# Key pages of the samples issued by SyncE between weights and value pages, in place of GpSimd

## Chip, cores and metric

The kernel runs on one core of a Trainium2 chip. The time is the device time of one execution in microseconds. Engines are called TensorE (PE), VectorE (DVE), ScalarE (ACT), GpSimd (POOL) and SyncE (SP); PEld is TensorE's loading of weights.

## The reference

One step of a decoder with two layers, for a prompt of 512 positions and 8 samples of one position each. Layer 0 mixes by gated linear attention and retention. Layer 1, in which the change lies, mixes by stick-breaking attention (8 heads of 128) and a gating of positions. For the samples the keys and values of the 2048 past positions come from a paged cache, 16 pages of 128 positions a sample:

```python
k_past = cache_k[i][page_table].reshape(dec_b, n_past, HC, DC)
v_past = cache_v[i][page_table].reshape(dec_b, n_past, HC, DC)
...
z = (jnp.einsum('bqhd,bshd->bhqs', q, k) * (q.shape[-1] ** -0.5)
     + offset.astype(jnp.float32)[None, :, None, None])
mask = (k_pos[None, :] < q_pos[:, None])[None, None]
log_beta = jax.nn.log_sigmoid(z)
log_rest = jnp.where(mask, jax.nn.log_sigmoid(-z), 0.0)
between = lax.cumsum(log_rest, axis=3, reverse=True) - log_rest
weight = jnp.where(mask, jnp.exp(log_beta + between), 0.0)
return jnp.einsum('bhqs,bshd->bqhd', weight, v)
```

All of it is in float32. A page of keys or of values, for all 8 heads, is 128 x 1024 numbers, 512 KB; there are 128 pages of each.

## The kernel before

**Projections.** A weight tile of 2048 x 128 is loaded in two halves of 512 KB (a half tile, 8 chunks of 128 rows). ScalarE casts each to `w_hi` (line 986) and VectorE subtracts to get `w_lo` (line 1384); this pair of operations is the split. TensorE multiplies `w_hi` by both parts of the activations and `w_lo` by one, 48 matmuls of 260 columns a half tile (line 558). `w_hi` and `w_lo` have two buffers each, so the split of half tile u waits for TensorE to finish u-2. The raw weights lie in a ring of four slots (`RING`, slots 1 to 4 of `raw`): SyncE loads half tile u+4 when u has been split (lines 375 and 376).

**Stages.** `ada0`, `ra` and `l0` (layer 0), `out0`, then `l1a` (4 passes of 8 half tiles: queries and one gate branch of layer 1), `l1b` (8 passes of 10 half tiles, one head a pass), `out1` (8 passes). The engines run the same order of half tiles, and between them the steps of a generator `mix`, in `l1b` the function `mix1` that each engine has its own version of.

**Samples.** Sample b's keys are multiplied by its queries on VectorE, in `key_page` (line 1773: eight multiply-and-sum instructions a page, one a head). That is done for sample 0 during `l1a`, at the steps of `KEYS0_AT`, and for sample i+1 during pass i of `l1b`, two pages at each step of `KEYS_AT`. The weighted sum of sample i's values runs on TensorE in pass i, two pages at each of the steps 3 to 10 (`value_pages(i, k)`, k from 0 to 7, at the end of the step; sixteen short matmuls of 256 columns). Pages of keys have three slots (`key_slot(p)` is p % 3), pages of values three others.

```python
KEYS0_AT = [23, 24, 24, 25, 25, 28, 28, 29, 30, 30, 31, 33, 33, 34, 34, 35]
KEYS_AT = [1, 3, 4, 5, 7, 8, 9, 10]
```

VectorE's semaphore `k_free` counts finished key pages, TensorE's `v_free` finished value pages. A page p of 3 or more is loaded once page p-3 is finished; the first three pages of a sample wait for the last pages of the sample before.

**Who loads.** SyncE issues the weights and the value pages, in the order of `l1b_pass`: a weight half tile at each `at_` from 0 to 9, value pages 1, 2, 0 at 0, and value pages 2at-3 and 2at-2 from 3 on. GpSimd issues the key pages, in order, and between them the queries of the sample (`queries`), the position weights (`head_weights`) and their bias (`head_bias`) of the head before. Each queue executes in its order: an instruction that waits holds all behind it.

In `walk` VectorE splits, in the turn of half tile u of `l1b`, half tile u+2, and takes the next step of `mix` behind it. ScalarE's `mix1` and TensorE's are interleaved in the same way; TensorE takes step k ahead of half tile k from step 2 on.

Of the kernel before, what the change touches and what calls it, by code (L numbers as in the profile page):

```python
# [24 lines left out]
NPAGE, PAGE, NPOOL = 16, 128, 160  # L25
# [23 lines left out]
L1A_ORDER = [TILE] * 4  # L49
# [18 lines left out]
KEYS0_AT = [23, 24, 24, 25, 25, 28, 28, 29, 30, 30, 31, 33, 33, 34, 34, 35]  # L68
KEYS_AT = [1, 3, 4, 5, 7, 8, 9, 10]
# [54 lines left out]
def build(nc, a, o, cst):  # L124
    ctx = ExitStack()
    with ctx:
        def sb(name, shape, dt=F32):
            return ctx.enter_context(nc.sbuf_tensor(name, shape, dt))
# [3 lines left out]
        def s(name):  # L132
            if name not in sems:
                sems[name] = ctx.enter_context(nc.semaphore(name))
            return sems[name]
# [22 lines left out]
        def region(n):  # L158
            at = used[0]
            used[0] += n  # L160
            assert used[0] <= 16600, used[0]
            return arena[:, at:at + n]
# [53 lines left out]
        qb = region(1024)  # L216
# [16 lines left out]
        ptab = sb("ptab", [1, NB * NPAGE], I32)  # L233
# [76 lines left out]
        def key_slot(p):  # L310

            return p % 3

        def key_buffer(slot):

            return raw[:, 0, :] if slot == 2 else pages[:, slot, :]

        def value_slot(p):

            return 2 + p % 3  # L320
# [38 lines left out]
        def _(sp):  # L359
# [19 lines left out]
            def load_tile(name, i, u, hh, w, col, turns=None):  # L379
                load(name, i, u, w[:, 8 * hh:8 * hh + 8, bass.ds(col, P)], turns)  # L380

            def load_mod(name, i, u, n, w, col, turns=None):
                load(name, i, u, w[:, 2 * n:2 * n + 2, bass.ds(col, 512)], turns)

            def weights(name, i, order, w_tile, tile_cols, mods=(), turns=None):
                seen = {TILE: 0, MOD: 0}
                for u in phases[name][3]:
                    kind = order[u // 2]
                    n = seen[kind]
                    seen[kind] += 1  # L390
                    if kind is TILE:
                        load_tile(name, i, u, n % 2, w_tile, tile_cols[n // 2], turns)
                    else:
                        w_mod, col = mods[n // 8]
                        load_mod(name, i, u, n % 8, w_mod, col, turns)

            v = {k: a[k][0].rearrange("(c p) n -> p c n", p=P)
                 for k in ("e_w_ada", "o_w_ada", "e_w_in", "o_w_in", "e_w_out", "o_w_out")}
# [17 lines left out]
            n = 24  # L416
# [31 lines left out]
            with sp.Fori(1, 8) as j:  # L448
                weights("out0", j, OUT_ORDER, v["e_w_out"], [j * 256, j * 256 + P], turns=(1, 8))

            def l1a_cols(j):
                return [(O_Q if j < 2 else O_VD) + (j % 2) * 512 + P * t for t in range(4)]

            for u in range(8):
                t, hh = OUT_FIRST[u] if u < 4 else (u // 2, u % 2)
                load_tile("l1a", 0, u, hh, v["o_w_in"], l1a_cols(0)[t])
            for j in range(1, 4):
                weights("l1a", j, L1A_ORDER, v["o_w_in"], l1a_cols(j))

            cv = a["cache_v"][0].rearrange("n s h d -> n s (h d)")  # L460

            def l1b_load(i, u):
                col = (O_K, O_V, O_GD, O_U, O_G)[u // 2]
                load_tile("l1b", i, u, u % 2, v["o_w_in"], i * P + col, (1, 8))

            def out1_load(u):
                t, hh = OUT1_FIRST[u]
                load("out1", 0, u, v["o_w_out"][:, 8 * hh:8 * hh + 8, P * t:P * t + P], None)

            def value_page(b, p):  # L470
                first = isinstance(b, int) and b == 0
                if p >= 3:
                    sp.wait_ge(s("v_free"), b * 16 + (p - 2))
                elif not first:
                    sp.wait_ge(s("v_free"), b * 16 - (0, 2, 1)[p])
                page = sp.value_load(ptab[0:1, bass.ds(b * NPAGE + p, 1)], min_val=0, max_val=NPOOL - 1)
                sp.dma_start(pages[:, value_slot(p), :], cv[bass.ds(page, 1)].rearrange("n s d -> (n s) d"))\
                    .then_inc(s(f"page{value_slot(p)}"), 16)

            def l1b_pass(i, last=False):  # L480
                for at_ in range(10):
                    if at_ < 6:
                        l1b_load(i, at_ + 4)
                    elif not last:
                        l1b_load(i + 1, at_ - 6)
                    else:
                        out1_load(at_ - 6)
                    if at_ == 0:
                        for p in (1, 2, 0):
                            value_page(i, p)  # L490
                    if at_ >= 3:
                        for p in (2 * at_ - 3, 2 * at_ - 2):
                            if p < NPAGE:
                                value_page(i, p)

            sp.wait_ge(s("ptab"), 16)
            for u in range(4):
                l1b_load(0, u)
            for i in range(8):
                l1b_pass(i, i == 7)  # L500
            with sp.Fori(1, 8) as j:
# [1508 lines left out]
        def layer1_pages(pool):  # L2010

            pool.wait_ge(s("ptab"), 16)
            pool.wait_ge(s("st_out"), 128)
            pool.wait_ge(s("s_out"), 128)
            ck = a["cache_k"][0].rearrange("n s h d -> n s (h d)")

            def key_page(b, p):
                first = isinstance(b, int) and b == 0
                page = pool.value_load(ptab[0:1, bass.ds(b * NPAGE + p, 1)], min_val=0, max_val=NPOOL - 1)
                if p >= 3:  # L2020
                    pool.wait_ge(s("k_free"), b * 16 + (p - 2))
                    pool.sem_inc(s("pool_waited"), 1)
                elif not first:
                    pool.wait_ge(s("k_free"), b * 16 - (0, 2, 1)[p])
                    pool.sem_inc(s("pool_waited"), 1)
                pool.dma_start(key_buffer(key_slot(p)), ck[bass.ds(page, 1)].rearrange("n s d -> (n s) d"))\  # L2026
                    .then_inc(s(f"key{key_slot(p)}"), 16)

            def queries(b):
                pool.dma_start(qb, q_dram[bass.ds(b, 1), :].rearrange("b n -> (b n)").partition_broadcast(P))\  # L2030
                    .then_inc(s("qb"), 16)

            def head_weights(h):
                if not (isinstance(h, int) and h == 0):
                    pool.wait_ge(s("oc"), h)
                    pool.sem_inc(s("pool_waited"), 1)
                pool.dma_start(ws, a["o_w_s"][0, bass.ds(h, 1)].rearrange("g t s -> t (g s)")).then_inc(s("ws_in"), 16)

            def head_bias(h):
                if not (isinstance(h, int) and h == 0):  # L2040
                    pool.wait_ge(s("gated"), h)
                    pool.sem_inc(s("pool_waited"), 1)
                if not (isinstance(h, int) and h == HC - 1):
                    pool.wait_ge(s("qb"), h * 32 + 32)
                    pool.sem_inc(s("pool_waited"), 1)
                pool.dma_start(brow[:, 0:P], a["o_b_s"][0, bass.ds(h, 1), :].rearrange("b n -> (b n)")
                               .partition_broadcast(P)).then_inc(s("qb"), 16)

            def sample_keys(b):
                for p in range(NPAGE):  # L2050
                    key_page(b, p)
                    if p == 1:
                        if isinstance(b, int) and b == 0:
                            pool.wait_ge(s("q_out"), 16)
                        if not (isinstance(b, int) and b < 2):
                            pool.wait_ge(s("qb"), b * 32 - 16)
                            pool.sem_inc(s("pool_waited"), 1)
                        queries(b)
                        if not (isinstance(b, int) and b == 0):
                            head_weights(b - 1)  # L2060
                    if p == 3 and not (isinstance(b, int) and b == 0):
                        head_bias(b - 1)

            sample_keys(0)
            sample_keys(1)
            with pool.Fori(2, NB) as b:
                sample_keys(b)
            head_weights(HC - 1)
            pool.wait_ge(s("qb"), 32 * HC - 16)
            head_bias(HC - 1)  # L2070
# [143 lines left out]
```

## Time and profile before

| | |
|---|---|
| time, median of 3 runs | 2187.14 us (2185.31 to 2188.33) |
| profiled execution | 2186.84 us, its span 2184.6 us |
| TensorE busy | 2080.9 us, 95% of the span |
| VectorE busy | 1151.6 us, 53% |
| ScalarE busy | 616.9 us, 28% |
| GpSimd busy | 201.7 us, 9% |
| moved by DMA | 445.40 MB, 204 GB/s in the mean |
| key pages | 128 of 512 KB, issued by GpSimd |
| value pages | 128 of 512 KB, issued by SyncE |

The span is the profiled time between the first and the last instruction. Busy time of an engine leaves out register, semaphore and DMA-issuing instructions. Idle time of an engine costs only where the end hangs on it.

### The profile page before, as it was taken

The numbers are of one execution on the slowest core, as the hardware profiler recorded it, in microseconds if no ns is written. First come the engines' busy times: TensorE is split into PE (matmuls) and PEld (weight loads), VectorE is DVE, ScalarE is ACT, GpSimd is POOL, SyncE is SP. The second block draws the span as 40 slices with busy tenths as digits, with TensorE's granted clock in tenths as the row PEclk, the third lists the DMA queues.
The fourth block names the chain that finished last, engine by engine and source line by source line (L and its number), as shares of the span: only waits on it lengthen the run. The fifth ranks groups of instructions, "written<-read, shape, count | busy, mean of one in ns | idle before, by whom it ended". The sixth has DMA issues, their size and how long they took to land.

```text
span 2184.6 us, 44372 instructions
## 1 busy us (share of the span) xinstructions
PE 2080.9 (95%) x16767; PEld 1841.3 (84%) x16767; DVE 1151.6 (53%) x3629; ACT 616.9 (28%) x793; POOL 201.7 (9%) x319
## 2 busy tenths in 40 slices
PE   6889999999999999899969998999999999998998
PEld 2258898988888888799969998888888888888997
DVE  1442544434454454644462277687777677745332
ACT  1422122121221212322233353323323323323221
POOL 0000101101010110100000011111111111000101
PEclk9989999999999999999989999999999999999999
DMA  9977665566675657343333367898898798763442
GB/s 324 305 224 251 194 196 183 186 193 214 192 215 180 209 181 224 103 117 112 113 139 87 108 193 256 288 296 283 285 308 291 257 311 286 229 201 92 131 133 64
DMA packets 401520, 445.40 MB, mean 204 GB/s; under 512 B 17141, under 2 KB 307279, under 8 KB 399808
## 3 DMA queue, kind: packets, MB, share of 16 engines
q1 hardware_dynamic: 359270, 311.99, 46.3%
q0 software_dynamic: 32288, 122.64, 16.1%
q10 hardware_dynamic: 9810, 8.73, 1.2%
q8 instruction: 97, 1.59, 0.3%
q14 instruction: 55, 0.44, 0.1%
HBM read 416.70 MB, written 26.61 MB: 203 GB/s over the span
## 4 chain that ended last, share of the span: by engine, by line
PE 80%; DVE 9%; ACT 4%; DMA 4%; issue 2%; SPq 0%; DVEq 0%; POOLq 0%; ACTq 0%; POOL 0%
PE pt L558 64%; PE m L558 13%; ACT arena L986 2%; DVE arena L1773 2%; DVE w_lo L1384 2%; ACT w_hi L986 2%; PE m L562 2%; DMA raw<-in_e_w_ada 1%; DMA arena<-in_o_k_norm_g 1%; DMA arena<-in_cache_v 1%; PE pt L562 1%; DVE arena L1943 1%; DMA arena<-in_cache_k 0%; DVE arena L1504 0%; DVE act_lo L1466 0%
## 5 line engine op out<-in xcount | busy, mean ns | idle before, releaser
L558 PE MATMUL pt<-act_hi,w_hi 128*128 128x260 f32 x4384 | 905.9, 288 | 29.1 <-DVE act_lo L1471 11.9
L558 PE MATMUL pt<-act_hi,w_lo 128*128 128x260 f32 x4384 | 887.0, 284 | 0.0
L558 PE MATMUL pt<-act_lo,w_hi 128*128 128x260 f32 x4384 | 885.8, 284 | 0.0
L1384 DVE TENSOR_TENSOR w_lo<-raw,w_hi 128x1024 fp32r<-128x1024 f32 x274 | 335.6, 1225 | 819.1 <-ACT w_hi L986 818.0
L558 PEld LDWEIGHTS pt<-act_hi,w_hi 128*128 128x128 f32 x4384 | 678.5, 190 | 90.9 <-issue 69.5
L558 PEld LDWEIGHTS pt<-act_lo,w_hi 128*128 128x128 f32 x4384 | 680.2, 190 | 0.0
L558 PEld LDWEIGHTS pt<-act_hi,w_lo 128*128 128x128 f32 x4384 | 680.1, 190 | 0.0
L986 ACT ACTIVATE w_hi<-raw 128x1024 fp32r<-128x1024 f32 x274 | 289.9, 1058 | 1104.1 <-PE pt L558 1088.2
L986 ACT ACTIVATE arena<-arena 128x1040 f32<-128x1040 f32 (+8 forms) x191 | 158.1, 837 | 164.4 <-DVE arena L1877 57.7
L1773 DVE CUSTOM_DVE_ANT_0 arena<-arena 128x128 f32<-128x128 f32 x704 | 155.1, 288 | 22.9 <-DMA arena<-in_cache_k 16.7
L558 PE MATMUL m<-raw,cond 128*9 128x512 f32 x768 | 131.2, 641 | 16.5 <-DMA raw<-in_e_w_ada 14.2
L558 PE MATMUL m<-arena 128*128 128x256 f32 (+6 forms) x704 | 115.4, 380 | 1.5 <-DVE arena L1617 1.5
L558 PEld LDWEIGHTS m<-arena 128*128 128x128 f32 (+4 forms) x704 | 74.5, 166 | 35.5 <-issue 18.5
L558 PEld LDWEIGHTS m<-raw,cond 128*9 128x9 f32 x768 | 16.6, 90 | 80.2 <-DMA raw<-in_e_w_ada 43.7
L1773 DVE CUSTOM_DVE_ANT_0 raw<-raw,arena 128x128 f32<-128x128 f32 x320 | 71.0, 288 | 13.0 <-DMA raw<-in_cache_k 13.0
L2026 POOL DMA_DIRECT2D arena<-in_cache_k x88 | 46.7, 531 | 334.5 <-DVE arena L1773 153.9
L562 PE MATMUL m<-c_ident,arena 128*128 128x128 f32 (+2 forms) x403 | 57.7, 275 | 19.0 <-DMA c_fold<-const_fold 8.9
L2113 POOL TENSOR_SCALAR arena<-arena 128x256 f32<-128x256 f32 x56 | 51.8, 925 | 226.2 <-DVE arena L1610 192.1
L558 PE MATMUL m<-arena,mod 128*8 128x256 f32 x1024 | 67.8, 380 | 2.5 <-ACT mod L986 1.5
L986 ACT ACTIVATE arena<-m 128x512 f32<-128x512 f32 (+2 forms) x93 | 49.8, 572 | 63.1 <-PE m L558 48.4
L562 PEld LDWEIGHTS m<-c_ident,arena 128*128 128x128 f32 (+2 forms) x403 | 44.7, 142 | 21.6 <-DMA c_fold<-const_fold 8.9
L558 PEld LDWEIGHTS m<-arena,ones 128*128 128x128 f32 x156 | 26.3, 196 | 24.3 <-issue 15.6
(174 smaller groups left out, 1209.7 us busy)
## 6 DMA issues: line engine op xcount, KB each, us to landing
arena<-in_cache_v SPq DMA_DIRECT2D x128, 512.0 KB, 5.2
raw<-in_o_w_in SPq DMA_DIRECT2D x112, 512.0 KB, 5.7
raw<-in_e_w_in SPq DMA_DIRECT2D x98, 512.0 KB, 4.6
raw<-in_e_w_ada SPq DMA_DIRECT2D x96, 512.0 KB, 5.7
raw<-in_o_w_ada SPq DMA_DIRECT2D x96, 512.0 KB, 5.2
arena<-in_cache_k POOLq DMA_DIRECT2D x88, 512.0 KB, 5.6
raw<-in_cache_k POOLq DMA_DIRECT2D x40, 512.0 KB, 5.6
raw<-in_e_w_out SPq DMA_DIRECT2D x32, 512.0 KB, 3.8
```

What stands on the lines that cost most here:

```text
L558: return pe.matmul(out, lhsT, rhs, start=start, stop=stop, skip_group_check=True)
L562: return pe.transpose(out, x, ident[0:k, 0:k])
L986: return act.activation(out, x, fn, **kw)
L1384: tt(w_lo[:, b, :], raw[:, sl, :], w_hi[:, b, :].bitcast(F32), ALU.subtract)\
L1773: last = dve.tensor_tensor_reduce(kpage, kpage, qb[:, P * h:P * h + P], 1.0, 0.0, ALU.mult, ALU.add, to[:, 8 * p + h:8 * p + h + 1])
L1943: tt(z, z, m012[:, 0:SB_ALL], ALU.subtract).then_inc(s("lw"), 1)
L2026: pool.dma_start(key_buffer(key_slot(p)), ck[bass.ds(page, 1)].rearrange("n s d -> (n s) d"))\
L2113: pool.tensor_scalar(carry[:, n, :], S[:, (n - 1) % 2, :], small[:, 6 * (n // 2) + n % 2:6 * (n // 2) + n % 2 + 1], None, ALU.mult).then_i ...
```

## The change

GpSimd's `key_page` goes to SyncE's queue. In `l1b_pass` the key pages of sample i+1 stand behind the weight load and ahead of the value pages of the same `at_` (but behind value pages 1, 2, 0 at 0): pages 0, 1, 2 at 0, and page p at `KEYS_AT[(p - 3) // 2]`, so 3 and 4 at 1, 5 and 6 at 3, 7 and 8 at 4, 9 and 10 at 5, 11 and 12 at 7, 13 and 14 at 8, 15 at 9. The pages of sample 0 stand between the loads of `l1a` and of the first half tiles of `l1b`. GpSimd keeps queries, position weights and bias, and issues those of a sample when all key pages of the sample before are finished. Slots, waits of each page and the work on the engines stay.

```diff
@@ -448,6 +448,32 @@
             with sp.Fori(1, 8) as j:
                 weights("out0", j, OUT_ORDER, v["e_w_out"], [j * 256, j * 256 + P], turns=(1, 8))
 
+            ck = a["cache_k"][0].rearrange("n s h d -> n s (h d)")
+
+            def key_page(b, p):
+                if p >= 3:
+                    sp.wait_ge(s("k_free"), b * 16 + (p - 2))
+                elif b > 0:
+                    sp.wait_ge(s("k_free"), b * 16 - (0, 2, 1)[p])
+                page = sp.value_load(ptab[0:1, b * NPAGE + p:b * NPAGE + p + 1], min_val=0, max_val=NPOOL - 1)
+                sp.dma_start(key_buffer(key_slot(p)), ck[bass.ds(page, 1)].rearrange("n s d -> (n s) d"))\
+                    .then_inc(s(f"key{key_slot(p)}"), 16)
+
+            def keys0(n):
+
+                if n == 16:
+                    sp.wait_ge(s("ptab"), 16)
+                    sp.wait_ge(s("st_out"), 128)
+                    sp.wait_ge(s("s_out"), 128)
+                for p in range(NPAGE):
+                    if n == (16 if p < 3 else KEYS0_AT[p - 3] * 8 // 9 + 6):
+                        key_page(0, p)
+
+            def keys1(b, at_):
+                for p in range(NPAGE):
+                    if at_ == (0 if p < 3 else KEYS_AT[(p - 3) // 2]):
+                        key_page(b, p)
+
             def l1a_cols(j):
                 return [(O_Q if j < 2 else O_VD) + (j % 2) * 512 + P * t for t in range(4)]
 
@@ -455,7 +481,9 @@
                 t, hh = OUT_FIRST[u] if u < 4 else (u // 2, u % 2)
                 load_tile("l1a", 0, u, hh, v["o_w_in"], l1a_cols(0)[t])
             for j in range(1, 4):
-                weights("l1a", j, L1A_ORDER, v["o_w_in"], l1a_cols(j))
+                for u in range(8):
+                    load_tile("l1a", j, u, u % 2, v["o_w_in"], l1a_cols(j)[u // 2])
+                    keys0(8 * j + u)
 
             cv = a["cache_v"][0].rearrange("n s h d -> n s (h d)")
 
@@ -485,17 +513,21 @@
                         l1b_load(i + 1, at_ - 6)
                     else:
                         out1_load(at_ - 6)
+                    if i == 0:
+                        keys0(32 + at_ + 4)
                     if at_ == 0:
                         for p in (1, 2, 0):
                             value_page(i, p)
+                    if not last:
+                        keys1(i + 1, at_)
                     if at_ >= 3:
                         for p in (2 * at_ - 3, 2 * at_ - 2):
                             if p < NPAGE:
                                 value_page(i, p)
 
-            sp.wait_ge(s("ptab"), 16)
             for u in range(4):
                 l1b_load(0, u)
+                keys0(32 + u)
             for i in range(8):
                 l1b_pass(i, i == 7)
             with sp.Fori(1, 8) as j:
@@ -2012,20 +2044,6 @@
             pool.wait_ge(s("ptab"), 16)
             pool.wait_ge(s("st_out"), 128)
             pool.wait_ge(s("s_out"), 128)
-            ck = a["cache_k"][0].rearrange("n s h d -> n s (h d)")
-
-            def key_page(b, p):
-                first = isinstance(b, int) and b == 0
-                page = pool.value_load(ptab[0:1, bass.ds(b * NPAGE + p, 1)], min_val=0, max_val=NPOOL - 1)
-                if p >= 3:
-                    pool.wait_ge(s("k_free"), b * 16 + (p - 2))
-                    pool.sem_inc(s("pool_waited"), 1)
-                elif not first:
-                    pool.wait_ge(s("k_free"), b * 16 - (0, 2, 1)[p])
-                    pool.sem_inc(s("pool_waited"), 1)
-                pool.dma_start(key_buffer(key_slot(p)), ck[bass.ds(page, 1)].rearrange("n s d -> (n s) d"))\
-                    .then_inc(s(f"key{key_slot(p)}"), 16)
-
             def queries(b):
                 pool.dma_start(qb, q_dram[bass.ds(b, 1), :].rearrange("b n -> (b n)").partition_broadcast(P))\
                     .then_inc(s("qb"), 16)
@@ -2046,25 +2064,25 @@
                 pool.dma_start(brow[:, 0:P], a["o_b_s"][0, bass.ds(h, 1), :].rearrange("b n -> (b n)")
                                .partition_broadcast(P)).then_inc(s("qb"), 16)
 
-            def sample_keys(b):
-                for p in range(NPAGE):
-                    key_page(b, p)
-                    if p == 1:
-                        if isinstance(b, int) and b == 0:
-                            pool.wait_ge(s("q_out"), 16)
-                        if not (isinstance(b, int) and b < 2):
-                            pool.wait_ge(s("qb"), b * 32 - 16)
-                            pool.sem_inc(s("pool_waited"), 1)
-                        queries(b)
-                        if not (isinstance(b, int) and b == 0):
-                            head_weights(b - 1)
-                    if p == 3 and not (isinstance(b, int) and b == 0):
-                        head_bias(b - 1)
-
-            sample_keys(0)
-            sample_keys(1)
+            def sample(b):
+                first = isinstance(b, int) and b == 0
+                if first:
+                    pool.wait_ge(s("q_out"), 16)
+                else:
+                    pool.wait_ge(s("k_free"), b * 16)
+                    pool.sem_inc(s("pool_waited"), 1)
+                if not (isinstance(b, int) and b < 2):
+                    pool.wait_ge(s("qb"), b * 32 - 16)
+                    pool.sem_inc(s("pool_waited"), 1)
+                queries(b)
+                if not first:
+                    head_weights(b - 1)
+                    head_bias(b - 1)
+
+            sample(0)
+            sample(1)
             with pool.Fori(2, NB) as b:
-                sample_keys(b)
+                sample(b)
             head_weights(HC - 1)
             pool.wait_ge(s("qb"), 32 * HC - 16)
             head_bias(HC - 1)
```

## Rows read from the trace of the kernel before

**Rows 1.** Busy time of each engine in a regular pass and in the longest.

```profile
core 0: us, PE busy (x) PEld busy (x) DVE busy (x) ACT busy (x) POOL busy (x), PEclk, DMA share, GB/s
...
1420.01:1500.30 80.29, 79.72 (x679) 69.88 (x680) 60.80 (x314) 26.65 (x35) 10.27 (x19) 1.00 0.88 288
...
1741.50:1823.93 82.43, 79.68 (x679) 69.75 (x679) 61.93 (x325) 26.23 (x34) 10.28 (x19) 1.00 0.87 291
```

**Rows 2.** Waits, 1100 to 1990 us: us in total, times, longest.

```profile
DVE arena L1773 <- DMA arena<-in_cache_k: 16.7, 12, 1.9
...
PE m L558 <- DMA arena<-in_cache_v: 1.0, 2, 0.6
```

**Rows 3.** Timeline of SyncE's issues: start us, us, line, transfer, how many.

```profile
1427.20 2.01 SPq L477 DMA_DIRECT2D arena<-in_cache_v  x2
...
1459.98 1.48 SPq L477 DMA_DIRECT2D arena<-in_cache_v  x2
...
1477.32 0.34 SPq L477 DMA_DIRECT2D arena<-in_cache_v  x1
```

**Rows 4.** Timeline of TensorE, passes 0 and 1; in brackets the idle time before.

```profile
1333.50 0.49 PE L558 MATMUL m<-arena,c_from_key 128*128 128x128 f32 x2 [2.91 <-DVE arena L1884]
...
1353.87 1.05 PE L558 MATMUL m<-arena,mod 128*8 128x256 f32 x16
...
1425.81 1.05 PE L558 MATMUL m<-arena,mod 128*8 128x256 f32 x16
...
1433.99 1.05 PE L558 MATMUL m<-arena,mod 128*8 128x256 f32 x16
...
1451.67 1.05 PE L558 MATMUL m<-arena,mod 128*8 128x256 f32 x16
...
1465.51 1.05 PE L558 MATMUL m<-arena,mod 128*8 128x256 f32 x16
...
1482.85 1.05 PE L558 MATMUL m<-arena,mod 128*8 128x256 f32 x16
```

**Rows 5.** Chain that ended last: two half tiles, start us, us.

```profile
1335.21 7.28 PE pt L558 x48
...
1459.64 5.94 PE pt L558 x48
```

**Rows 6.** Timeline of VectorE, and ScalarE's cast at 1425.98.

```profile
1351.55 1.23 DVE L1384 TENSOR_TENSOR w_lo<-raw,w_hi 128x1024 fp32r<-128x1024 f32 x1 [2.85 <-ACT w_hi L986]
...
1425.98 1.06 ACT L986 ACTIVATE w_hi<-raw 128x1024 fp32r<-128x1024 f32 x1 [1.42 <-PE pt L558]
...
1428.62 1.22 DVE L1384 TENSOR_TENSOR w_lo<-raw,w_hi 128x1024 fp32r<-128x1024 f32 x1
...
1430.84 0.28 DVE L1773 CUSTOM_DVE_ANT_0 raw<-raw,arena 128x128 f32<-128x128 f32 x1
...
1434.23 0.08 DVE L1773 DVE_READ_ACCUMULATOR2_ANT arena<- 128x1 f32 x1
...
1443.31 0.68 DVE L1921 COPY arena<-m 128x512 f32<-128x512 f32 x1
...
1467.58 0.08 DVE L1773 DVE_READ_ACCUMULATOR2_ANT arena<- 128x1 f32 x1
...
1481.96 0.28 DVE L1773 CUSTOM_DVE_ANT_0 arena<-arena 128x128 f32<-128x128 f32 x1
```

**Rows 7.** Landing of SyncE's pages 1453 to 1461.5, all of them, all of GpSimd's.

```profile
DMA to landing us min/median/max: 4.4/4.9/5.4
...
DMA to landing us min/median/max: 3.2/5.2/8.6
...
DMA to landing us min/median/max: 3.4/5.6/8.6
```

**Rows 8.** Busy time and granted clock (PEclk) in stretches of 5 us.

```profile
1335.00:1340.00 5.00, 5.00 (x31) 5.00 (x31) 5.00 (x35) 0.76 (x3) 1.07 (x2) 0.66 0.67 208
...
1350.00:1355.00 5.00, 2.84 (x27) 1.41 (x26) 2.37 (x4) 2.54 (x5) 0.00 (x0) 1.00 0.89 302
```

## Prediction

> **What bounds the kernel now.** I read the page first, whose busy shares are in the table above: TensorE is busy nearly throughout, so the kernel gets faster only by as much as TensorE idles, and slower by whatever makes it wait. Then the busy time by stage. The change touches the end of `l1a` and the eight mixing passes of `l1b`. A regular pass takes 80.3 us with TensorE busy for 79.7; the worst takes 82.4 [rows 1]. The lists of waits say who holds whom: VectorE waits 16.7 us in all for key pages in the two arena slots, TensorE 1.0 us in all for value pages [rows 2]. So little can be won: the 2.1 us by which the worst pass exceeds a regular one, and the 0.6 us that TensorE idles in a regular one.
>
> **What the change moves.** 128 key page loads leave GpSimd's queue for SyncE's. All but three begin with a wait on `k_free`, and SyncE executes in order, so what counts is what stands behind each wait: in a pass, weight loads and value pages.
>
> *Weights.* A load reuses the ring place of the half tile four before it. Four half tiles of 5.9 us [rows 5], less a landing of at most 8.6 [rows 7], leave a load some 15 us to be late. A key wait ends at most a half tile and a pair of key pages (5.9 and 3.5 us) after SyncE comes to it. Cost nothing, and the same cover serves `l1a`, where no value page is queued. At the start of a pass value pages 1, 2, 0 go ahead of the keys: nothing again.
>
> *Value pages.* They have no such cover. SyncE issues value pages 2at-3 and 2at-2 behind the keys of the same `at_`. Now pages 3 and 4 go out at 1427.20, and page 3 is read at 1434.5 (halfway through the sixteen short matmuls of 1433.99); pages 11 and 12 go out at 1459.98, and page 11 is read at 1466.0; page 15 goes out at 1477.32 and is read at 1483.4 [rows 3, 4]. Landing in 4.4 to 5.4 us [rows 7], they have 1 to 3 us to spare.
>
> Now the key waits ahead of them. Page p waits until VectorE has finished page p-3, and it is placed at the `at_` whose number is VectorE's step for that page. But SyncE reaches `at_` once split `at_` is done, and VectorE starts step `at_` only behind split `at_`+1, a half tile later. So SyncE stands until VectorE has finished the pair, and issues the second key page and the first value page only then. After VectorE's end come: 0.9 us from release to issue (SyncE's of 1427.20 follows TensorE's release, halfway through the matmuls of 1425.81, by that much), 1.1 us to SyncE's next issue (two in 1.48 us, of which 0.34 is one), and 5.3 us to land as the second of two (4.4 to 5.4 us in a stretch in which GpSimd issued no page) [rows 3, 4, 7]. Sum 7.3 us. Place by place, in the times of the pass shown [rows 4, 6]:
>
> - at 3, value page 3: VectorE ends keys 2 and 3 at 1434.3, so the page is there at 1441.6 against a need at 1434.5: 7.0 us. VectorE could run 1.3 us sooner here (its split began at 1428.62, the cast it needs had ended at 1427.04), which leaves **5.7**.
> - at 4, value page 5: keys 4 and 5 start at about 1436.7 (a split and three short instructions behind keys 3) when page 4 isn't waited for, and end 3.5 later; the page is there at 1447.4 and would be read at about 1442.7, plus the delay just found: hidden by a us.
> - at 5, value page 7: keys 6 and 7 start at 1443.9 and end 3.5 later; 1454.7 against 1452.2: **2.5**.
> - at 7, value page 11: end 1467.6, there at 1474.9, needed at 1466.0: **8.9**.
> - at 8, value page 13: TensorE has just waited for page 11 and has a half tile ahead of it, VectorE is through: hidden by more than 5.
> - at 9, value page 15: key page 15 waits for page 12 alone, done at 1482.0 plus 1.7; 1491.0 against 1483.4: **7.6**.
>
> One stall doesn't pay for the next: VectorE's steps hang on splits that TensorE's half tiles release, so its lag behind each half tile is the same however long TensorE stood before. Sum 24.7 us a pass.
>
> *The clock.* In pass 0 TensorE stops for 2.91 us at 1333.5. From 1335 to 1340 the granted clock is 0.66, so part of them ran at 1.2 GHz in place of 2.4, and the half tile took 7.28 us in place of 5.94; from 1350 to 1355, with 2.2 us idle, the clock is 1.00 [rows 4, 5, 8]. Three stops a pass are of 5.7 us and more, and each costs another 1.34: 4.0 a pass. From below that is nothing, from above I take double.
>
> *Against it.* The queries now go out at once when the last page of the sample is free, without two key pages ahead of them, so the 0.6 us goes. A pass: 24.7 + 4.0 - 0.6 = 28.1 us.
>
> Passes 1 to 6 pay this: 168.6. In pass 0 VectorE is earlier against page 3: its keys end at 1348.7, the page is there at 1356.0, needed at 1354.4 [rows 4, 6]: 1.6. I take 2.8 at page 5 (what page 3 no longer hides), nothing at 7, then 8.9, 7.6 and two clock drops: 23.6. Pass 7 loads no keys: nothing. The worst pass gives its 2.1 back. 168.6 + 23.6 - 2.1 = 190 us on a span of 2184.6 is 2374.7; with the 2.2 us that the execution (2186.84) has around its span, **2377** us. That execution lies 0.3 us under the median of the runs, so nothing is to be corrected.
>
> *What gets cheaper.* Pages on SyncE's queue land in 5.2 us in the median, on GpSimd's in 5.6 [rows 7]. VectorE would wait less for keys, but it isn't what sets the end: nothing. The Trainium skill, "DMA: Bandwidth & Descriptors", Issuing engine by pattern, calls the path of SyncE generally faster than GpSimd's. The medians agree, by 0.4 us; by that rule alone the change costs nothing or gains. The same page, Queues, rings and completion order, says that an engine takes turns between queues and drains each in order: by it a value page stands behind the key page, not beside it. The pair of 4.4 and 5.4 us agrees, and it would be 5.3 by this rule, as I take, and 4.4 without it.
>
> **Rivals.**
> *Milder.* The same waits, but the clock holds and pages land faster, the transfers being spread over longer passes. At 4.4 us each of four places costs 0.9 less: 24.7 - 3.6 - 0.6 = 20.5 a pass, about 139 in all with pass 0, so 2326; at 3.2, the quickest landing [rows 7], about 106, so 2293. For it: the lighter traffic. Against: the second page of a pair on SyncE's queue. Chance 12%.
> *Heavier.* Key, value and weight loads of one queue hold each other up to landings of 7.4 us (the longest is 8.6 [rows 7]), and page 5 is no longer hidden: about 41 a pass with the clock, 280 in all, 2467; doubled clock cost alone makes 2405. Chance 8% above 2420.
> *Faster.* Key pages land earlier, VectorE idles a quarter of each pass [rows 1], and it finishes each pair before SyncE comes to the wait. Value pages go out when they do now, and the kernel wins the 2.1 and 0.6 in each of 7 passes: 2181. It decides where VectorE's pair ends 7.3 us ahead of TensorE's need. At page 11 that is 9 us sooner than now, before the half tile of 1459.64 [rows 5] has begun, and its step follows a split that the half tile before that one releases; so it needs VectorE's order to be another than I read. Chance 4%, and 2% that stalls and gains cancel.
> *Forecast*: 74%, and 2330 to 2415 is what its own terms allow.
>
> What leaves out 2 in 10 is 2310 to 2420. Faster than before by over 0.2% 0.04, within 0.2% (about what a measurement of this kernel can tell from no change) 0.02, slower 0.94.
>
> **What the changed profile would show.** Regular passes of 108 us where 80.3 are now; TensorE held by `in_cache_v` for some 170 us, in about 28 stops, the longest of each pass ahead of value pages 11 and 15; SyncE waiting for VectorE's `k_free` ahead of value pages; the granted clock under 1.00 in the passes; VectorE's waits for `in_cache_k` nearly gone; nothing changed before 1300 us and in the last 200. If TensorE is not held by value pages, I have SyncE's order wrong, and the prediction falls. If it is and a pass takes under 95 us, the landing or the clock was priced too high.

## The result and the profile after

The changed kernel takes 2385.77 us in the median of 4 runs (2382.99 to 2386.65), the kernel before 2187.73 (2185.31 to 2190.38). The ratio is 1.090 with a 95% interval of 1.0883 to 1.0917: slower by 198 us. Forecast were 2377 us, 2310 to 2420. One later run of the kernel before took 4057 us and stands outside every comparison here.

The busy share of each engine, from the page of the changed kernel:

```profile
PE 2127.3 (89%) x16767; PEld 1863.6 (78%) x16767; DVE 1151.0 (48%) x3629; ACT 616.8 (26%) x793; POOL 132.5 (6%) x190
```

TensorE executes the same 16767 matmuls but is busy for 46 us more, and idle for another 154 us. Busy time by stretch, two passes of `l1b` and the last one, which loads no keys (columns as in [rows 1]):

```profile
1434.74:1543.23 108.49, 86.16 (x680) 72.72 (x680) 61.26 (x318) 26.32 (x34) 1.61 (x3) 0.89 0.66 216
1543.23:1652.96 109.73, 87.10 (x680) 73.40 (x680) 61.17 (x318) 26.30 (x34) 1.60 (x3) 0.89 0.63 212
...
2089.84:2171.00 81.16, 79.21 (x678) 69.64 (x677) 33.69 (x60) 24.98 (x32) 1.07 (x2) 1.00 0.54 159
```

A pass with key pages takes 108.4 to 110.1 us where it took 80.3 [rows 1]; in the six of them TensorE is idle for 22.8 us in the mean and busy for 86.4, with a granted clock of 0.87 to 0.89 over the pass where it was 1.00. The pass without key pages takes 81.2 us, much as a regular one did. The lists of waits, 1290 to 2190 us, of TensorE, SyncE and VectorE:

```profile
PE m L590 <- DMA arena<-in_cache_v: 156.6, 29, 9.2
...
SPq L458 <- DVE mod L1805: 243.0, 44, 17.3
SPq L458 <- DVE arena L1805: 201.9, 41, 17.3
...
DVE raw L1805 <- DMA raw<-in_cache_k: 0.4, 1, 0.4
```

TensorE was held by value pages for 1.0 us before [rows 2], now for 156.6, in 29 stops. SyncE stands for 445 us at line 458, which is the wait of a key page for VectorE. VectorE hardly waits for key pages any more, where it waited 16.7 us for those in the arena slots [rows 2] and 13.0 us for those in the raw slot (list of waits before, 1100 to 1990 us):

```profile
DVE raw L1773 <- DMA raw<-in_cache_k: 13.0, 8, 2.9
```

What the change makes cheap is what set nothing.

The four stops of pass 1, from TensorE's timeline (idle time before each in brackets), which answer to [rows 4]:

```profile
1466.70 1.04 PE L590 MATMUL m<-arena,mod 128*8 128x256 f32 x8 [5.11 <-DMA arena<-in_cache_v]
...
1488.28 0.62 PE L590 MATMUL m<-arena,mod 128*8 128x256 f32 x8 [2.18 <-DMA arena<-in_cache_v]
...
1510.98 1.04 PE L590 MATMUL m<-arena,mod 128*8 128x256 f32 x8 [8.68 <-DMA arena<-in_cache_v]
...
1536.73 1.04 PE L590 MATMUL m<-arena,mod 128*8 128x256 f32 x8 [6.36 <-DMA arena<-in_cache_v]
```

They stand ahead of value pages 3, 7, 11 and 15. Behind them lies this order in SyncE's timeline, here at 3, 7 and 9 (it answers to [rows 3]):

```profile
1458.81 0.35 SPq L459 DMA_DIRECT2D raw<-in_cache_k  x1
1460.50 0.36 SPq L459 DMA_DIRECT2D arena<-in_cache_k  x1
1461.62 1.45 SPq L505 DMA_DIRECT2D arena<-in_cache_v  x2
...
1502.87 0.33 SPq L459 DMA_DIRECT2D raw<-in_cache_k  x1
1504.60 0.33 SPq L459 DMA_DIRECT2D arena<-in_cache_k  x1
1505.70 1.44 SPq L505 DMA_DIRECT2D arena<-in_cache_v  x2
...
1531.37 0.33 SPq L459 DMA_DIRECT2D arena<-in_cache_k  x1
1532.47 0.33 SPq L505 DMA_DIRECT2D arena<-in_cache_v  x1
```

and in VectorE's, the last multiply-and-sum of keys 3 and of keys 9:

```profile
1459.47 0.29 DVE L1805 CUSTOM_DVE_ANT_0 arena<-arena 128x128 f32<-128x128 f32 x1
...
1503.54 0.29 DVE L1805 CUSTOM_DVE_ANT_0 arena<-arena 128x128 f32<-128x128 f32 x1
```

Read from the last row up: VectorE ends keys 9 at 1503.83 (1503.54 and 0.29); SyncE issues the second key page 0.8 us later, the value pages 1.1 us after that at 1505.70, and TensorE goes on at 1510.98, 5.3 us on. That is 7.2 us behind VectorE where the prediction had 7.3.

### The profile page after: what moved, and what is told of

Its sections match the earlier page's. It is cut to its first block, busy times and chain, and to the rows that moved or that the text cites. A ratio compares the mean times of both kernels' runs of the same rounds, so it can differ in the third digit from the quotient of the medians.

```text
span 2384.9 us, 44152 instructions
## 1 busy us (share of the span) xinstructions
PE 2127.3 (89%) x16767; PEld 1863.6 (78%) x16767; DVE 1151.0 (48%) x3629; ACT 616.8 (26%) x793; POOL 132.5 (6%) x190
## 4 chain that ended last, share of the span: by engine, by line
PE 73%; DVE 11%; DMA 8%; ACT 4%; issue 2%; SPq 2%; DVEq 0%; ACTq 0%; POOLq 0%
PE pt L590 59%; PE m L590 13%; DMA arena<-in_cache_v 6%; DVE arena L1805 2%; ACT w_hi L1018 2%; DVE w_lo L1416 2%; ACT arena L1018 1%; DMA raw<-in_e_w_ada 1%; DVE raw L1805 1%; PE m L594 1%; DMA arena<-in_o_k_norm_g 1%; DVE arena L1860 1%; SPq L458 1%; SPq L504 1%; PE pt L594 0%
## 5 line engine op out<-in xcount | busy, mean ns | idle before, releaser
L590 PE MATMUL m<-arena,mod 128*8 128x256 f32 x1024 | 81.9, 420 | 156.6 <-DMA arena<-in_cache_v 156.6
L590 PEld LDWEIGHTS m<-arena,mod 128*8 128x8 f32 x1024 | 18.7, 88 | 188.8 <-DMA arena<-in_cache_v 171.2
L590 PE MATMUL m<-arena 128*128 128x256 f32 (+6 forms) x704 | 128.2, 400 | 1.5 <-DVE arena L1649 1.5
L590 PEld LDWEIGHTS m<-arena 128*128 128x128 f32 (+4 forms) x704 | 80.9, 176 | 44.9 <-issue 29.2
L590 PEld LDWEIGHTS m<-raw,cond 128*9 128x9 f32 x768 | 16.7, 91 | 82.0 <-DMA raw<-in_e_w_ada 43.9
L590 PEld LDWEIGHTS m<-arena,ones 128*128 128x128 f32 x156 | 29.1, 217 | 28.0 <-issue 19.5
```

Of the source, the lines that this page charges most:

```text
L590: return pe.matmul(out, lhsT, rhs, start=start, stop=stop, skip_group_check=True)
```

## The experiments

The first four take the change apart. In two only the order of SyncE's issues differs, in one SyncE has the waits without the transfers, in one a single place is turned round.

**Value pages first.** The same queue, transfers and waits; from 3 on the value pages of an `at_` go ahead of its key pages:

```diff
-                    if not last:
-                        keys1(i + 1, at_)
                     if at_ >= 3:
                         for p in (2 * at_ - 3, 2 * at_ - 2):
                             if p < NPAGE:
                                 value_page(i, p)
+                    if not last:
+                        keys1(i + 1, at_)
```

> The changed kernel, but from at 3 on the value pages of an at are issued ahead of its key pages and not behind them. Same queue, same waits, same transfers. Theory (value pages stand behind waits for VectorE): the four stops a pass on value pages go, a regular pass takes 80 us again, 2180 to 2190 us. Rival (it is the traffic of all pages on one queue that slows the value pages): the stops stay in the main, over 2300 us.

Measured: 2187.6 us in the median of 12 runs (2184.0 to 2192.13) beside 2187.99 for the kernel before; ratio 0.9999, 0.9987 to 1.0011. TensorE's wait for value pages in its list:

```profile
PE m L590 <- DMA arena<-in_cache_v: 2.8, 6, 0.8
```

All 198 us are gone with the order of two statements, though SyncE's queue still carries every page. The rival, traffic on one queue, falls.

**Keys one `at_` later**, but still ahead of the value pages:

```diff
-                    if at_ == (0 if p < 3 else KEYS_AT[(p - 3) // 2]):
+                    if at_ == (0 if p < 3 else KEYS_AT[(p - 3) // 2] + 1):
...
                         for p in (2 * at_ - 3, 2 * at_ - 2):
                             if p < NPAGE:
                                 value_page(i, p)
+                if not last:
+                    keys1(i + 1, 10)
```

> The changed kernel, but key pages 3 to 15 are issued one at later (2, 4, 5, 6, 8, 9 and the start of the next pass), still ahead of the value pages of that at. Theory (SyncE comes to the wait a half tile ahead of VectorE's step): one at later the wait is a half tile shorter, the value pages go out within 1 us of where they went in the kernel before, 2180 to 2195 us. Rival (any key page ahead of a value page is too much, as it adds its issue and its transfer): stops of 1 to 3 us at four places, 2210 to 2270 us.

Measured: 2185.23 us in the median of 12 runs (2180.16 to 2189.67), ratio 0.999, 0.9977 to 1.0004. TensorE's list from 1290 us on has no wait for a value page at all. So a key page ahead of a value page costs nothing measurable at these places; what costs is that SyncE comes to its wait a half tile before VectorE comes to the step. The median lies 2.8 us under the kernel before, but the interval takes in no change: it isn't shown to beat it.

**The waits alone**, in the kernel before; GpSimd issues all key pages as ever:

```diff
+                    if not last:
+                        for p in range(3, NPAGE):
+                            if at_ == KEYS_AT[(p - 3) // 2]:
+                                sp.wait_ge(s("k_free"), (i + 1) * 16 + (p - 2))
                     if at_ >= 3:
                         for p in (2 * at_ - 3, 2 * at_ - 2):
```

> The kernel before, with GpSimd issuing all key pages as it does there, but SyncE waits for k_free at the places at which the changed kernel has its key pages 3 to 15, without loading anything. Theory (the wait costs, not the transfer): the stops are those of the changed kernel less 1.1 us each for the issue that is missing, about 18 us a pass and 5 to 6 for the clock, 2320 to 2365 us. Rival (the transfer ahead in the queue costs): within 20 us of the kernel before, 2187 to 2207 us.

Measured: 2361.19 us (4 runs), ratio 1.0804, 1.078 to 1.0827: 173 of the 198 us without a single load moved to another queue. TensorE's wait for value pages:

```profile
PE m L562 <- DMA arena<-in_cache_v: 137.1, 29, 8.5
```

It is 19.5 us less than in the changed kernel over 29 stops, 0.7 each; the missing issue of 1.1 us is partly taken back by landing, which is 6.0 us in the median for all value pages, on the page's list of transfers, against 5.6 in the changed kernel.

**Order turned round at 7 alone**, in the changed kernel:

```diff
-                    if not last:
+                    if not last and at_ != 7:
                         keys1(i + 1, at_)
                     if at_ >= 3:
...
+                    if not last and at_ == 7:
+                        keys1(i + 1, at_)
```

> The changed kernel with the order turned round at 7 alone: value pages 11 and 12 ahead of key pages 11 and 12. The stop of 8.7 us on value page 11 goes. Theory with the cover counted: value page 13 at 8 was hidden by that stop only; VectorE ends keys 10 and 11 at about 66 us of the pass, the page is there 7.3 later against a need at 69.8, so a stop of about 3.8 us appears on value page 13 and the gain is 4.9 us a pass and up to 2.2 for the clock: 2336 to 2351 us. Rival (each place stands by itself): 8.7 and 2.2 in each of 7 passes, 2310 us.

Measured: 2304.71 us (4 runs), ratio 1.0542, 1.0516 to 1.0569. My expectation missed by 31 us, the rival's 2310 was near. But the stops, from TensorE's timeline in pass 1, are not what the rival says either:

```profile
1453.30 0.98 PE L592 MATMUL m<-arena,mod 128*8 128x256 f32 x8 [4.84 <-DMA arena<-in_cache_v]
...
1474.11 0.62 PE L592 MATMUL m<-arena,mod 128*8 128x256 f32 x8 [1.58 <-DMA arena<-in_cache_v]
...
1501.43 1.04 PE L592 MATMUL m<-arena,mod 128*8 128x256 f32 x8 [2.86 <-DMA arena<-in_cache_v]
1512.66 0.62 PE L592 MATMUL m<-arena,mod 128*8 128x256 f32 x8 [2.69 <-DMA arena<-in_cache_v]
```

The stop of 8.7 us is gone, and one of 2.9 us has come up on value page 13, where I had counted 3.8. The stop on value page 15, though, has shrunk from 6.4 to 2.7 us. The chain that ended last shows why, from half tile 8 to value page 15:

```profile
1492.28 5.76 PE pt L592 x48
...
1498.12 1.06 ACT w_hi L1020
...
1504.06 1.72 DVE arena L1807 x16
...
1507.60 5.01 DMA arena<-in_cache_v
```

VectorE's keys 12 (1504.06) hang on the split that half tile 8 (1492.28) releases. The new stop, from 1498.6 to 1501.43, lies behind that half tile and ahead of the need, so it gives the time to VectorE and takes it off the next stop. By this one case, a stop between the release and the need is shared with the next; one ahead of the release is not.

The other four have the order of the first experiment, and the key pages first at one `at_` only, 3, 5, 7 or 9 (here 7):

```diff
-                    if not last:
+                    if not last and at_ == 7:
                         keys1(i + 1, at_)
                     if at_ >= 3:
...
+                    if not last and at_ != 7:
+                        keys1(i + 1, at_)
```

> The order with the value pages first everywhere (2187.6 us), and key pages 5 and 6 ahead of value pages 3 and 4 at 3 alone. One stop a pass, on value page 3: VectorE ends keys 2 and 3 as late as in the kernel before, since no other stop gives it a lead, so 6 to 7 us and 1.5 to 2.2 for the clock in passes 1 to 6 and about 1.5 in pass 0: 2230 to 2245 us. If a stop at 9 and 7 gives VectorE no lead at 3, as the prediction's sum has it up to 1.3 us, the stop is the 5.1 us of the changed kernel: under 2232 us.

> Value pages first everywhere but at 5: key pages 9 and 10 ahead of value pages 7 and 8. One stop of 2.2 to 2.5 us a pass, on value page 7. If so short a stop leaves the clock alone: 7 times 2.3, 2202 to 2206 us. If every stop costs 1.3 us more by the clock: 2211 to 2216 us.

> Value pages first everywhere but at 7: key pages 11 and 12 ahead of value pages 11 and 12. One stop of 8.7 us on value page 11 in each of 7 passes, and 1.3 to 2.2 for the clock: 2258 to 2265 us. If the stops shorten one another in the changed kernel, this single one is longer than 8.7 us and the time above 2268 us.

> Value pages first everywhere but at 9: key page 15 ahead of value page 15. One stop of 6.4 to 7.6 us on value page 15 in each of 7 passes, and 1.3 to 2.2 for the clock, less 0.6 a pass for the lead of VectorE at the sums of later: 2238 to 2252 us. With the three others of this call, the sum over 2187.6 us is 198 us if the four places add up as in the changed kernel; far above 200 us if they shorten one another there.

Measured, each in 4 runs beside 2186.12 us for the kernel before (6 runs):

| keys first at | median us | ratio and interval | over before, us | TensorE's waits for value pages, us |
|---|---|---|---|---|
| 3 | 2240.72 | 1.0251, 1.0233 to 1.0270 | 54.6 | 42.0 |
| 5 | 2206.34 | 1.0091, 1.0073 to 1.0109 | 20.2 | 17.6 |
| 7 | 2263.62 | 1.0359, 1.0341 to 1.0378 | 77.5 | 61.3 |
| 9 | 2243.99 | 1.0268, 1.0249 to 1.0287 | 57.9 | 50.9 |

All four are in or within a us of the expected ranges. One stop of each, from TensorE's timeline of the kernel with keys first at 3:

```profile
1533.35 1.04 PE L592 MATMUL m<-arena,mod 128*8 128x256 f32 x8 [6.51 <-DMA arena<-in_cache_v]
```

at 5:

```profile
1456.29 0.62 PE L592 MATMUL m<-arena,mod 128*8 128x256 f32 x8 [2.22 <-DMA arena<-in_cache_v]
```

at 7:

```profile
1578.80 1.04 PE L592 MATMUL m<-arena,mod 128*8 128x256 f32 x8 [8.57 <-DMA arena<-in_cache_v]
```

and at 9:

```profile
1498.28 1.04 PE L592 MATMUL m<-arena,mod 128*8 128x256 f32 x8 [6.80 <-DMA arena<-in_cache_v]
```

The four add up to 210 us, the changed kernel has 198, so the places nearly add up. Of the 12 us between, 10 are the place at 3: in the mean of passes 1 to 6 its stop is 6.7 us alone and 5.0 in the changed kernel. The stops have given VectorE a lead there, as its split ahead of keys 2 and 3 shows, first in the changed kernel and then with keys first at 3 only:

```profile
1454.06 1.22 DVE L1416 TENSOR_TENSOR w_lo<-raw,w_hi 128x1024 fp32r<-128x1024 f32 x1 [0.41 <-ACT w_hi L1018]
...
1520.53 1.22 DVE L1418 TENSOR_TENSOR w_lo<-raw,w_hi 128x1024 fp32r<-128x1024 f32 x1
```

In the first VectorE stands idle for 0.4 us until ScalarE's cast is there; in the second it comes 1.3 us after the end of the cast (1519.27), from other work. The stop at 7 isn't needed for that: with the order turned round there, the stop at 3 is 5.0 us as well. Which of the others gives the lead was not tested.

The last column against the one before it gives the clock and what else changes: with keys first at 5 the stops explain all but 2.6 us, with keys first at 7 there are 16 us more than the stops, 2.3 a pass, at 3 there are 12.6 and at 9 only 7.0. At 9 a small wait goes at the same time, that of TensorE for `mod`, once a pass, some 15 us behind value page 15. The lists of the kernel before, of keys first at 7 and at 9, and of the changed kernel:

```profile
PE m L558 <- DVE mod L1890: 5.1, 8, 0.7
...
PE m L592 <- DVE mod L1924: 4.5, 8, 0.6
...
PE m L592 <- DVE mod L1924: 0.7, 1, 0.7
...
PE m L590 <- DVE mod L1922: 0.4, 1, 0.4
```

## Why the prediction was right

The mechanism was that of the forecast, and so was nearly every size. By the steps of the prediction:

- *Weights and `l1a` cost nothing.* Right: TensorE waits for no weight half tile in its list, and the first 1300 us are near enough unchanged (TensorE busy for 1223.2 us in them, 1225.4 before; all of the difference arises in the first 400 us, long ahead of the first key page). The last pass takes 81.2 us.
- *SyncE reaches the wait a half tile before VectorE's step, and the value pages stand behind.* Shown by the two kernels that differ in order alone, and by the waits without transfers, which cost 173 of the 198 us.
- *7.3 us behind VectorE's end.* 7.2 measured at value page 11: 0.8, 1.1 and 5.3. At value page 15 of the same pass it is 6.1 (0.7, 1.1 and 4.3): the page landed sooner than the 5.3 that I had put for every place.
- *The stops.* 5.7, 2.5, 8.9 and 7.6 us forecast; over the six passes 1 to 6 the stops are 4.6 to 5.3, 1.9 to 2.4, 8.2 to 8.8 and 6.4 to 8.3. Their sum was put at 24.7 us a pass and is 22.8: (156.6 - 19.9 of pass 0) / 6. The stops on value pages 5 and 13 are hidden, as said. The lead at page 3 was read too short: the cast had ended at 1427.04 and the split began at 1428.62, which is 1.6 us and not 1.3; alone and in the changed kernel the stops differ by 1.7.
- *Pass 0.* 20.9 us of stops forecast, 19.9 measured, as 1.2, 0.6, 1.5, 9.2 and 7.4; of the 2.8 put at page 5, 0.6 lie there, and 1.5 at page 7, where I had none.
- *The clock.* Mis-sized: 4.0 us a pass forecast, 6.7 measured, as the rise of TensorE's busy time from 79.7 to 86.4 us in the mean of six passes with the same matmuls. I had priced it by the half tile behind one stop of 2.9 us. Pass 0 has the same fault: of the 46 us that TensorE is busy longer, 40 lie in passes 1 to 6 and 6 in pass 0, where 2.7 were forecast. That too little and the stops' 1.9 us too much nearly cancel, which is luck: 28.1 us a pass forecast, 28.9 measured (109.2 against 80.3). From the end of one pass's short matmuls to the same place six passes on the changed kernel takes 655.1 us where 484.6 were needed, 170.5 more; forecast were 166.5 (168.6 less 2.1).
- *One stall doesn't pay for the next.* True of the stops of the changed kernel but for the lead at 3, which the sum had. Wrong as a general sentence: the kernel turned round at 7 shows a stop on value page 13 that shortens the one on page 15. There I had kept the sum's rule for page 15 and missed by 31 us.
- *The 0.6 us that go.* Right in size, but the cause given is not what removes them. They are TensorE's waits for `mod`, 5.1 us before and 0.4 in the changed kernel. The queries, issued at once, were to do it; but with keys first at 7 only they go out at once too and 4.5 us are left, while with the waits alone, where GpSimd's order is the old one, 0.7 are left. These waits are gone (0.4 to 0.7 us) in every kernel with a stop on value page 15, and stay (2.5 to 5.1) in every one without.
- *What gets cheaper is worth nothing.* Right: VectorE's waits for key pages fall from 16.7 us [rows 2] to none in the arena slots and from 13.0 to 0.4 in the raw slot, and TensorE gains nothing from it. The 2.1 us of the worst pass seem to have come back, too: no pass stands out beyond two kinds, of 108.6 and of 109.8 us, which alternate for a reason that is not known.

The rivals: one queue's traffic was tested and costs nothing measurable; the faster outcome needed VectorE to be ahead of SyncE, and SyncE waits 445 us for it. The milder one needed the clock to hold and quicker landing: the clock fell, and the value pages at the stops of pass 1 landed in 5.0 to 5.2 us, that on page 15 in 4.2, where 4.4 was its price. The heavier one needed landings of 7.4 us; its 41 us a pass are also more than its terms give (28.1, four times 2.1 and some 2.5 for page 5 and its clock make 39).

## What to carry to other kernels

A queue that serves two consumers makes the tighter one wait for whatever the other's transfers wait for: before a load with a wait is moved, ask which loads stand behind it and how many us each can spare, and put those with little to spare ahead. A place in an order that is written out by hand must be named by when the issuing engine comes to it, not by the number of the step at which the other engine does the work: here the two differed by one half tile, which was the whole loss. When a stop is removed, look for the one that it hid, and ask between which two events VectorE, or whoever is late, was given the time.

## What the runs showed of the hardware

Key pages of 512 KB landed sooner from SyncE's queue than from GpSimd's. The landing of all key pages, issued by SyncE, in the changed kernel, and of all its value pages:

```profile
DMA to landing us min/median/max: 3.1/4.3/8.1
...
DMA to landing us min/median/max: 3.3/5.6/7.9
```

Key pages landed in 5.6 us in the median from GpSimd's queue [rows 7] and land in 4.3 here, while the value pages, now second behind them, went from 5.2 to 5.6. That is not all the queue: with GpSimd issuing and passes nearly as long (the waits alone) the key pages land in 5.2 us in the median, and with SyncE issuing in passes of 80 us in 5.1 (value pages first) and 5.3 (one `at_` later). The Trainium skill, "DMA: Bandwidth & Descriptors", Issuing engine by pattern, calls SyncE's path generally faster than GpSimd's; these traces agree, by 1.3 us between the two kernels, but only by 0.9 where both have passes of over 100 us, and by 0.3 to 0.5 where both have passes of 80; the rest is the lighter traffic of longer passes. It was worth nothing.

The clock costs more than the stop that drops it suggests. Busy time and granted clock of the changed kernel in stretches of 5 us, behind the stops that end at 1466.7, 1488.3 and 1511.0:

```profile
1465.00:1470.00 5.00, 3.30 (x18) 2.45 (x19) 2.03 (x20) 0.00 (x0) 0.00 (x0) 0.50 1.04 331
1470.00:1475.00 5.00, 5.00 (x41) 5.00 (x41) 0.00 (x0) 0.00 (x0) 0.00 (x0) 0.95 0.93 345
...
1485.00:1490.00 5.00, 2.82 (x30) 1.64 (x29) 4.85 (x8) 0.37 (x1) 0.00 (x0) 1.00 0.96 335
...
1510.00:1515.00 5.00, 4.02 (x14) 2.03 (x15) 0.00 (x0) 0.00 (x0) 0.00 (x0) 0.51 1.04 373
1515.00:1520.00 5.00, 5.00 (x39) 4.67 (x38) 0.00 (x0) 0.00 (x0) 0.00 (x0) 1.00 0.93 337
```

Behind the stops of 5.1 and 8.7 us the granted clock is 0.50 and 0.51 up to the end of the stretch, so TensorE runs at 1.2 GHz for some 4 us of its work, and at 2.4 GHz (0.95 and 1.00) in the stretch after that; behind the stop of 2.2 us it stays at 2.4 GHz. Four us of work at half the clock are 2 us lost. The half tile behind the first stop, from the chain that ended last:

```profile
1467.74 7.24 PE pt L590 x48
```

It takes 7.24 us in place of 5.94, and the short matmuls ahead of it are slow as well, so a stop costs 2.2 us by the clock (6.7 over three) rather than the 1.34 read from one half tile alone.
